# Gated linear recurrence: masked level products side by side, summed by TensorE

## The reference

```python
f = lbh + (1.0 - lbh) * jax.nn.sigmoid(z)          # forget gate
k = (1.0 - lbh) * jax.nn.sigmoid(-z)
def step(S, inp):                                   # per chunk of tokens
    G = jnp.cumsum(gc, axis=2)                      # gc = log f
    o_inter = jnp.einsum('bhtk,bhkv->bhtv', qc * jnp.exp(G), S)
    diff = G[:, :, :, None, :] - G[:, :, None, :, :]
    decay = jnp.exp(jnp.where(causal[:, :, None], diff, -jnp.inf))
    A = jnp.einsum('bhtsk,bhsk->bhts', qc[:, :, :, None, :] * decay, kc)
    o = o_inter + jnp.einsum('bhts,bhsv->bhtv', A, vc)
    S = jnp.exp(G_last[:, :, 0, :])[..., None] * S + jnp.einsum('bhsk,bhsv->bhkv', kc * jnp.exp(G_last - G), vc)
o = _rms_norm(o, hg_norm) * jax.nn.silu(hg)
```

## Time and profile before

| | us |
|---|---|
| median of 3 runs | 3068.36 |
| the profiled execution | 3066.06, its span 3064.3 |
| TensorE busy | 2883.0 (94%) |
| VectorE busy | 1530.9 (50%) |
| ScalarE busy | 699.3 (23%) |
| GpSimd busy | 574.7 (19%) |

### The profile page before, as it was taken

How to read it: one execution, slowest core, us unless ns; L and a number is a source line. 1 busy time by engine, 2 the same in 40 slices (tenths; PEclk the granted TensorE clock), 3 DMA queues, 4 the chain that set the end, 5 groups by cost and what they waited for, 6 DMA issues and landing times. The chain is left out here.

```text
span 3064.3 us, 50934 instructions
## 1 busy us (share of the span) xinstructions
PE 2883.0 (94%) x19321; PEld 2789.7 (91%) x19321; DVE 1530.9 (50%) x3429; ACT 699.3 (23%) x1351; POOL 574.7 (19%) x330
## 2 busy tenths in 40 slices
PE   8999999999699986999989988869989999999998
PEld 7999999999699974999959987869979999999998
DVE  5333322223767639999944767657344222333323
ACT  5111111111323225221113444331031111111111
POOL 0122121112311102212131211122002111122220
PEclk9999999999799999999999988889999999999999
DMA  4111111111223111243262241324211111111111
GB/s 127 42 54 56 41 55 41 41 41 41 76 65 121 38 59 49 91 133 121 94 176 63 57 145 58 93 74 147 68 48 56 42 41 41 41 55 54 41 34 57
DMA packets 239302, 212.94 MB, mean 69 GB/s; under 512 B 26978, under 2 KB 216578, under 8 KB 239042
## 3 DMA queue, kind: packets, MB, share of 16 engines
q1 hardware_dynamic: 228866, 180.78, 19.8%
q10 hardware_dynamic: 6336, 18.88, 1.6%
q0 software_dynamic: 3968, 11.54, 1.3%
HBM read 167.94 MB, written 43.21 MB: 69 GB/s over the span
## 5 line engine op out<-in xcount | busy, mean ns | idle before, releaser
L271 POOL TENSOR_TENSOR ff_wlo<-ff_raw,ff_whi 128x1024 fp32r<-128x1024 f32 x124 | 298.4, 2426 | 1202.3 <-ACT ff_whi L369 1201.6
L567 DVE TENSOR_TENSOR ff_prod<-ff_silu,ff_gu 128x384 f32<-128x384 f32 x132 | 68.8, 521 | 806.8 <-ACT ff_silu L374 806.8
L97 PE MATMUL ff_dn<-ff_ahi,ff_whi 128*128 128x384 f32 (+1 forms) x1056 | 340.7, 323 | 8.0 <-DVE ff_alo L573 3.8
L97 PE MATMUL ff_gu<-front_hhi,ff_whi 128*128 128x384 f32 (+1 forms) x1056 | 340.9, 323 | 2.6 <-DVE front_hlo L511 2.3
L99 PE MATMUL ff_gu<-front_hhi,ff_wlo 128*128 128x384 f32 (+1 forms) x1056 | 339.7, 322 | 0.0
L98 PE MATMUL ff_gu<-front_hlo,ff_whi 128*128 128x384 f32 (+1 forms) x1056 | 339.7, 322 | 0.0
L99 PE MATMUL ff_dn<-ff_ahi,ff_wlo 128*128 128x384 f32 (+1 forms) x1056 | 339.6, 322 | 0.0
L98 PE MATMUL ff_dn<-ff_alo,ff_whi 128*128 128x384 f32 (+1 forms) x1056 | 339.5, 322 | 0.0
L97 PE MATMUL ff_gu<-rear_hhi,ff_whi 128*128 128x384 f32 (+1 forms) x1056 | 339.1, 321 | 0.0
L99 PE MATMUL ff_gu<-rear_hhi,ff_wlo 128*128 128x384 f32 (+1 forms) x1056 | 338.8, 321 | 0.0
L98 PE MATMUL ff_gu<-rear_hlo,ff_whi 128*128 128x384 f32 (+1 forms) x1056 | 338.8, 321 | 0.0
(11 more groups left out here) (336 smaller groups left out, 6184.9 us busy)
## 6 DMA issues: line engine op xcount, KB each, us to landing
ff_raw<-in_ffn_w_gate SPq DMA_DIRECT2D x44, 512.0 KB, 3.7
ff_raw<-in_ffn_w_up SPq DMA_DIRECT2D x44, 512.0 KB, 3.7
ff_raw<-in_ffn_w_down SPq DMA_DIRECT2D x44, 512.0 KB, 3.4
scratch_feat<-sel_stage ACTq DMA_DIRECT2D x32, 528.0 KB, 2.7
sel_raw<-in_w_in SPq DMA_DIRECT2D x28, 512.0 KB, 3.7
merge_gates<-scratch_feat SPq DMA_DIRECT2D x48, 176.0 KB, 2.7
tok_raw<-in_w_in SPq DMA_DIRECT2D x8, 1024.0 KB, 6.4
mix_pages<-in_cache_k SPq DMA_DIRECT2D x52, 128.0 KB, 2.4
```

What stands on the lines that cost most here:

```text
L97: nc.tensor.matmul(out, w_hi, x_hi, start=first, stop=False)
L271: nc.gpsimd.tensor_tensor(wlo[:, u, :], raw[:, u % RAW, :], whi[:, u, :], ALU.subtract).then_inc(w_lo_done, 1)
L567: nc.vector.tensor_tensor(prod[:, 0:w], act_out[:, b, 0:w], gu[:, b, 1, 0:w], ALU.mult).then_inc(prod_done, 1)
```

## The change

Placing by predicated copy becomes a multiply of a whole bank half by a 0/1 mask into `attn`, which now keeps the products side by side (`HALF_AT` is where a half begins); `outputs` sums them: each level's 64 columns go by a product of their own to the late columns of the output. The ring has four banks; `kd_ps` and `st_ps` share a bank. `turn` of the next chunk is issued inside `outputs`, ahead of its last half. All idle products in units go, except three ahead of every second sample-state product (60 before the first unit).

```diff
-            def chunk(h, n):
-                        if y < NL:
-                            place = nc.vector.copy_predicated(half(at, y, 1), blocks(mask, y), blocks(product, y))
...
+            def mask(h, n):
+                w = P if n < TILES else NS
+                for i, x in halves_of(n):
+                    dve.wait_ge(pairs_done, HALVES * h + i + 1)
...
+                    if n < TILES:
+                        c = (4 if x == 0 else NL - 3) * HD
+                        last = nc.vector.tensor_tensor(to[:, 0:c], product[:, 0:c], kept[:, 0:c], ALU.mult)
...
+                    last.then_inc(masked, 1)
```

```diff
             def turn(h, n):
...
                 wait(pe, kdT_ready, TT * h + n)
+                wait(pe, S_ready, TILES * h + n)
...
+            def outputs(h, n, nxt):
+                o, kept = o_ps[:, 0:w], attn[0:w, n % 2 if n < TILES else 2, :]
                 wait(pe, o_kept, TT * h + n)
+                carried = 0 < n < TILES
+                if carried:
                     pe.wait_ge(S_ready, TILES * h + n)
+                    nc.tensor.matmul(o, S[:, (n + 1) % 2, :], q_in[:, tile(n)], start=True, stop=False)
+                order = halves_of(n) if carried else halves_of(n)[::-1]
+                for i, x in order:
+                    if nxt and (i, x) == order[-1]:
+                        turn(*nxt)
+                    pe.wait_ge(masked, masked_through(h, i))
+                    for y, lo, c in products_of(n, x)[::1 if carried else -1]:
+                        part = kept[:, HALF_AT[x] + lo:HALF_AT[x] + lo + c]
+                        if y == NL:
+                            last = nc.tensor.matmul(o, hv[0:w, n, :], part, start=not carried, stop=carried)
+                        else:
+                            last = nc.tensor.matmul(half(o, y, 1), hv[0:w, n, :], blocks(part, y), start=False, stop=(n == 0 and y == 1))
...
                 if n == TILES:
...
                     for b in range(DB):
+                        if b % 2 == 0:
+                            idle_products(nc, pairs[:, 3, 0:P], ident, 3)
```

`following(h, u, after)` pairs each chunk with the next, the next unit's first chunk included, so products and masks run on over a unit's end. TensorE and VectorE:

```diff
-                idle_products(nc, kd_ps[:, P:2 * P], ident, 12)
...
+            def unit(h, u, after, before, beyond):
+                for n, nxt in following(h, u, after):
+                    last = n == CHUNKS_OF[u][-1]
+                    if nxt and not last:
+                        pair_products(*nxt)
+                    outputs(h, n, None if last else nxt)
+                    if nxt and last:
+                        ready(*after)
+                        pair_products(*nxt)
+                        turn(*nxt)
+                    if nxt:
+                        states(*nxt)
+                    if not after and n >= TILES - 1:
+                        end_sums(n - TILES + 1)
+                    if before and n == CHUNKS_OF[u][0]:
+                        sums(*before)
```

ScalarE: j 0 square, total decay, scaled keys, decays 0; j 1 decays 2 to 5; j 2 inverse root, decays 6; j 3 decays 1; then `keep_kd` of the next chunk and `keep_o`; at the last chunk `keep_o`, `logs(beyond)`, `keep_kd`. The keys are loaded to a buffer of their own:

```diff
-                nc.scalar.activation(kk[:, COLS[u]], kL[:, LATE, COLS[u]], ACT.Ln, bias=tiny[:, 0:1]).then_inc(kk_logged, 1)
+                nc.scalar.activation(kk[:, COLS[u]], k_in[:, COLS[u]], ACT.Ln, scale=omlb[:, DynSlice(h, 1)],
+                                     bias=tiny[:, 0:1]).then_inc(kk_logged, 1)
+            def scaled_keys(h, u):
+                wait(act, pairs_done, halves_through(h - 1, CHUNKS_OF[u][-1]))
```

The own values are loaded once for all heads by eight DMAs into a cleared `own_v` (NS x 4096 columns, memset by GpSimd), in place of VectorE's product per head:

```diff
+                    for b in range(DB):
+                        rows = slice(DT * b, DT * (b + 1))
+                        sp.dma_start(own_v[rows, :, b, :], hv_d[SEQ + DT * b:SEQ + DT * (b + 1), 0:HG * P
+                                                                ].rearrange("s (h v) -> s h v", v=P)).then_inc(own_in, 16)
```

The sample states' products now go to `sum_ps`. The last unit's normalisation is split in two, columns 512 to 1023 and the 32 sample columns (`ENDS`), each with its own square, sum, root and store, and runs on VectorE with GpSimd's gate product ahead:

```diff
+            def end_norm(x):
+                cols, at = ENDS[x]
+                dve.wait_ge(rooted, LAST + x + 1)
+                nc.vector.tensor_tensor(tmp[:, at], root[:, at], root[:, at], ALU.mult).then_inc(tail_step, 1)
...
+                nc.vector.tensor_tensor(rec[:, cols], rec[:, cols], tmp[:, at], ALU.mult).then_inc(rec_ready, 1)
```

More of the change, by code:

```diff
@@ L2623, in norm, with unit @@
                                                ALU.mult).then_inc(normed, 1)
-            def unit(h, u, after, before):
-                for j, n in enumerate(CHUNKS_OF[u]):
-                    chunk(h, n)
+            def unit(h, u, after, before, beyond):
+                for j, (n, nxt) in enumerate(following(h, u, after)):
+                    if n < TILES:
+                        state(h, n)
+                    else:
+                        if not after:
+                            end_variance(0)
+                        new_states(h)
+                    last = n == CHUNKS_OF[u][-1]
+                    if after and j == 0:
+                        distances(*after, (0, 2, 3))
@@ L2628, in unit @@
                     if before and j == 1:
                         variance(*before)
+                    if after and j == 1:
+                        distances(*after, (5,))
+                    if after and j == 2:
+                        queries(*after, (2, 3, 4))
+                    if before and j == 3:
+                        factor(*before)
+                    if u == 1 and j == 3:
+                        decayed_states(h)
+                    if beyond and last:
+                        forget(*beyond)
@@ L2630, in unit @@
+                    if after and j == 3:
+                        queries(*after, (6,))
+                    if nxt and not last:
+                        mask(*nxt)
                     if after and j == 0:
-                        forget(*after)
+                        distances(*after, (4,))
                     if after and j == 1:
-                        scan(*after)
-                        distances(*after, (0, 2))
+                        distances(*after, (6,))
+                        carried_queries(*after)
@@ L2635, in unit @@
                     if after and j == 2:
[L2636 to L2640 removed]
+                        queries(*after, (5, 7))
                     if after and j == 3:
[L2642 to L2643 removed]
+                        queries(*after, (1,))
@@ L2654, in _ @@
             carried_queries(0, 0)
-            queries(0, 0, range(1, NL))
+            queries(0, 0, (*range(2, LATE + 1), LATE + 1, 1))
+            forget(0, 1)
+            mask(0, 0)
             dve.wait_ge(gain_in, 16)
             nc.vector.tensor_scalar(gain[:, 1:2], gain[:, 0:1], float(P) ** -0.5, None, ALU.mult).then_inc(gain_ready, 1)
+            scan(0, 1)
             heads_one_by_one(unit)
-            variance(HG - 1, 1)
-            factor(HG - 1, 1)
-            norm(HG - 1, 1)
+            end_norm(0)
+            end_variance(1)
+            end_norm(1)
         @block.tensor
```

346 lines of the change are left out of this document (193 added, 153 removed).

## The result

The changed kernel takes 3063.42 us as the median of its four executions, which lie far apart: 3034.74, 3043.10, 3083.74 and 3085.47. Kernel before beside it: 3068.86. The ratio compares the two lower ones with the fast runs of before, since the two upper ones had a lower TensorE clock (0.945 against 0.959 and 0.963 over the span): 0.9906, 95% interval 0.9889 to 0.9922, so 29 us faster; between the medians of all runs lie only 5 us. The forecast was 60 us less than before, with 3040 as the upper end. The direction was right; time and size were wrong. What follows is read from the profiled execution of 3043.10 us (span 3041.4, 22.9 less than before).

The account below looks back on a forecast made before the run. VectorE's order, then idle products at a low clock, bound the recurrence. Savings of 64.3, 1.1 and 4.5 us, less 8 and 2 for clock, took profiled 3066.1 to 3006; 2.3 more gave 3009 us, range 2998 to 3025.

Parts of the forecast that it names:

- Placing: Per chunk, masked multiplies of 256 and 320 columns replace eight copies: 0.9 us for 2.0 to 2.3; VectorE saves 50.
- TensorE's sums: Each chunk's output becomes 16 passes at 0.11 us instead of 2: 1.5 us more; steady chunk 4.1 us.
- Units at the full clock: Four units of four chunks (u0) at 18.9 us, four of five (u1) at 25.3: 176.8 for the recurrence, not 241.1.
- The lateness at u0's end: At the end of each head's four-chunk unit, the next unit's level 6 and 1 queries come 1.1 us late.
- The hold of VectorE beside GpSimd: VectorE steps with two SBUF inputs slow beside GpSimd; one query held some 0.9 us, 4 us in all.
- The end: From the last kept output to the last store, 12.0 us become 7.5: 4.5 saved, bounds 2 and 7.
- The front: Before the recurrence's first product, earlier key fetch and a log not waiting for scaling: 1.1 us sooner, bounds 0 and 1.5.
- Clock: Without idle products, half the units get a 4 us clock fall: 8 us plus 2 for handovers, bounds 0 and 24.
- Rival C: Without filler the recurrence's clock drops; 140 us at 0.50 eat the 70 us gain, near 3170 us; chance 0.05.
- A: VectorE's order still stalls each chunk, 1 us for 32 chunks, plus clock falls: 3049 or 3040 us; chance 0.16.
- B: Stepped writes into PSUM make output passes slow, 0.21 us each, adding 46 us: 3055 us; chance 0.04.
- D: No gain: VectorE's wait moves whole to the ScalarE copy or a load: 3068 us; chance 0.03.

Follow-up runs that it names:

- after: The changed kernel as first measured, against the kernel before: median 3063.42 us, ratio 0.9906; its profiled execution took 3043.10 us.
- order-alone kernel: Changed kernel with reset loaded before keys, own-values memset after GpSimd's first loads, level 6 and 1 queries first, no idle product added: 3111.72 us.
- best kernel: Changed kernel plus those order edits, float32 512-column idle products in sample chunks and chunks 0 and 1, bf16 ones in other prompt chunks: 3016.52 us.

## Why the prediction was wrong

**Right, by its own steps.** Placing: 455 ns a masked multiply. VectorE does 34 us less in the stage for 50 forecast: the copies had been 67 us, 1.9 a chunk where the sum took the upper 2.3, and the queries grew from 421 to 561 ns. That costs nothing, as VectorE is not the bound. TensorE's sums: 0.105 to 0.107 us a pass, pitch 4.08. Turn: 0.37 us at a unit's front for 0.5. Units at the full clock: 19.43 and 25.56 for 18.9 and 25.3, which makes 181.4 for 176.8. The lateness at u0's end: 0.77 us at most in after and 1.06 with the bf16 products, for 1.1, and by its reason, since moving the queries cut it to under 0.5. The hold of VectorE beside GpSimd is in after as well (time lines of both engines):

```profile
1886.30 1.58 DVE L2606 TENSOR_TENSOR hg_qL<-hg_q,hg_f 128x272 f32<-128x272 f32 x1
...
1886.17 1.40 POOL L2355 TENSOR_TENSOR hg_sq<-hg_sq,hg_var 128x544 f32<-128x544 f32 x1
```

The Trainium skill's page "SBUF — State Buffer", section "Who interferes with whom", says that a VectorE instruction with two SBUF inputs contends with a GpSimd one that reads SBUF, and the trace agrees: 1.58 us against 0.42 alone. The refine on GpSimd pays too, 1903 ns for 1294.

**Terms that were off by a little.** The end: 6.2 us saved for 4.5, inside its bounds; its last rows are

```profile
2026.98 0.69 DVE L2690 TENSOR_TENSOR hg_rec<-hg_rec,hg_sq 128x512 f32<-128x512 f32 x1
...
2027.70 1.88 SPq L2340 DMA_DIRECT2D scratch_mixed<-hg_rec  x2
```

The front had the wrong sign: 1.3 us longer for 1.1 shorter. I counted the fetch of the keys one issue earlier as a gain and did not follow what it was moved past: the reset, which the scan needs; and I costed the memset only by what waits behind it on GpSimd, not by what VectorE does beside it. Undoing the reset alone showed nothing, as the memset's hold then filled the time; the memset alone was not undone. With both undone the front came to 16.3 us, which is before's own: the 1.1 us of the forecast showed in no run.

**The step that failed** is "Clock", in its words: "A fall lasts about 4 us and costs 2 ... I give half of the units a fall: 8 us, and 2 more for handovers. Bounds 0 and 24." It measured 42 us. The number of falls was not the error, there were four; their length was, 10 to 44 us, which is 99 us at 0.50 in place of 16. Two things were wrong with the 4 us. First, they came from one fall, the one behind the wait of 1.07 us, and it is the shortest of eight in the trace of before. Windows over three of them, then over the stage:

```profile
1846.50:1860.50 14.00, 14.00 (x55) 11.58 (x54) 4.83 (x14) 1.80 (x6) 1.26 (x1) 0.51 0.61 195
1877.50:1887.50 10.00, 6.48 (x28) 6.19 (x29) 7.39 (x22) 3.55 (x12) 2.73 (x3) 0.50 0.00 0
1904.50:1908.00 3.50, 3.32 (x16) 3.23 (x16) 3.50 (x11) 2.74 (x10) 0.55 (x1) 0.52 0.03 7
...
1796.31:2037.43 241.12, 207.07 (x1480) 193.03 (x1480) 169.94 (x495) 91.42 (x279) 35.17 (x28) 0.86 0.24 74
```

The eight together are 68 us at 0.50. The window of 5.00 us in the earlier trace rows lies within the second, so even idle products did not end a fall at once. Four falls of the mean 8.5 us would have cost some 15 us, still inside the upper bound of 24. Second, I carried a length over to a kernel without the idle products, and that is the larger part. That these make the difference is shown from both sides: put back into after they bring 99 us at 0.50 down to 14 (time steady within 10 us), taken out of before they raise 68 us to 190. That the clock makes the time is shown by the head of 81.87 us against 45.0, in which the work is the same.

Rival C had the mechanism and its break-even: the gain is eaten from 140 us at 0.50 (some 155 by the 0.43 us measured for each). In the profiled execution of after the mean clock of the stage, weighted from the windows by unit, is 0.78, some 99 us at 0.50, which leaves 23 us of gain. In the two executions near 3085 us it was presumably more than that (clock 0.945; they have no trace), and in the traced run of the order-alone kernel it was nearly the whole stage. I gave C 0.05 because the waits that preceded falls were to go. But one wait can be enough when nothing brings the clock back: the traced run of the order-alone kernel has fewer waits than after, and behind one of 2.26 us stood 299 us at 0.50. The Trainium skill, page "TensorE: Matmul & The Clock Gate", section "A second HAM failure mode: psum-queue depth-cycling", puts such swings down to short pauses between groups of products. Here the pauses don't tell the stretches apart: 0.7 us of pauses in the head of 81.87 us at 0.50, 1.7 and 2.2 us in the first heads of the best kernel at 1.00. The measurement decides.

**The other rivals.** A is refuted by the doubled multiplies, B by the pass of 0.105 us, D by the stage itself: that the median, 3063.42 us, lies near D's 3068 is chance, since the wait D feared did not come.

**What stays open.** Of the falls, those at head 0's first u1 go by its wait: with 1.34, 1.70, 1.75, 2.26 and 3.51 us the clock fell, with 0.45, 0.92 and 1.07 it did not. At the stage's front the wait alone does not decide: 1.25, 1.27 and 2.64 us were followed by a fall in kernels without idle products in the units, 1.43, 2.15 and 2.24 us were not in those with eight, with bf16 and with wide ones. In after the fall of 1937 followed a wait of 0.77 us, and the same wait at 1890.87 had none behind it. Those in sample chunks follow no wait over 0.4 us, and what makes them is not settled; nor is what raises the clock. In after it rose behind the sums' products on 512 and 272 columns; in the order-alone kernel the same ones ran at 0.50 and it did not rise. The traces of the four kernels with float32 idle products on 512 columns have 7 to 38 us at 0.50 in the stage, the four that compute everything with bf16 ones alone 62 to 79, after 99; with one trace each, that is a tendency and not a rule. The 4-column products are not to blame. Why one program falls in one execution and not in the next, no run here shows.

## What to carry to other kernels

Ask of every idle product that a change removes what it did for the clock, and read the length of a fall from all falls of the stage, not from one; even so it holds only for a stretch that is built like them. When TensorE becomes the bound, the clock it could do without becomes the largest term. When several executions of one kernel differ by tens of microseconds, look at the granted clock by windows of the stage before explaining the median. A little idle work in few places is worth trying before a lot everywhere: with six wide products a head four executions took 3012 to 3023 us, with the order alone 3031 to 3130.

## What the hardware showed that I had not expected

- TensorE stayed at 1.2 GHz through whole heads in which it was busy for 81.14 of 81.87 us, with float32 passes mostly of 64 and 128 columns.
- An idle product on 512 columns costs 0.87 us in float32 and 0.22 in bf16, at the full clock.
- A VectorE step on 4 columns takes 2.85 us when it begins beside a GpSimd memset of 32x4096, and ends with it.
